# Second-product tiles of the MLPs: from 13 matmuls over 512 tokens to 24 over 256, with their weight blocks 64 bytes higher

## The reference, cut to what matters

```python
def sq_relu_mlp(h, w1, w2):
    a = jax.nn.relu(h @ w1)      # 1024 -> 4096
    return (a * a) @ w2          # 4096 -> 1024, added to x
```

## Time and profile before

| what | value |
|---|---|
| median of 3 runs | 2172.73 us (2171.98 to 2174.36) |
| the profiled execution | 2172.76 us, of which the traced span is 2171.0 us |
| PE | 2157.3 us busy (99%), 12440 matmuls |
| PEld | 1860.9 us (86%), 12440 loads |
| DVE / ACT / POOL | 1494.3 us (69%) / 998.5 us (46%) / 14.5 us (1%) |
| mean granted PE clock | 0.998 |

### The profile page before, as it was taken

The page is one execution under the profiler, slowest core; times in us unless marked ns, Lnnn a source line. Parts: engine busy times, 40 slices in busy tenths (PEclk is TensorE's granted clock), DMA queues, the critical chain, the costliest instruction groups (busy, mean ns, idle before and its releaser), DMA issues.

```text
span 2171.0 us, 32587 instructions
## 1 busy us (share of the span) xinstructions
PE 2157.3 (99%) x12440; PEld 1860.9 (86%) x12440; DVE 1494.3 (69%) x2518; ACT 998.5 (46%) x1724; POOL 14.5 (1%) x14
## 2 busy tenths in 40 slices
PE   9999999999999999999999999999999999999998
PEld 8887888888778888888898899998888888899997
DVE  5866665558666567586666777776887658777775
ACT  5445533434446344375554544444434435444444
POOL 0000000000000000200000000000000000000000
PEclk9999999999999999999999999999999999999999
DMA  5655443335645433464354333333233213333331
GB/s 199 184 176 164 152 128 106 113 122 180 190 138 155 127 103 113 132 181 153 117 155 137 97 98 98 117 98 104 91 92 112 88 49 100 102 100 107 98 114 52
DMA packets 136699, 268.21 MB, mean 124 GB/s; under 512 B 21773, under 2 KB 79931, under 8 KB 136160
## 3 DMA queue, kind: packets, MB, share of 16 engines
q1 hardware_dynamic: 136544, 266.13, 39.7%
HBM read 235.37 MB, written 26.77 MB: 121 GB/s over the span
## 4 chain that ended last, share of the span: by engine, by line
PE 98%; DVE 1%; ACT 0%; issue 0%; DMA 0%; DVEq 0%; SPq 0%; ACTq 0%
PE ps L2348 30%; PE ps L2349 30%; PE ps L2354 29%; PE ps L2369 2%; PE ps L2380 2%; PE ps L2352 1%; PE ps L2351 1%; PE ps L2404 0%; PE ps L2406 0%; PE ps L2394 0%; PE ps L2405 0%; PE ps L2393 0%; PE ps L2392 0%; PE ps L2423 0%; DVE t_X L3066 0%
## 5 line engine op out<-in xcount | busy, mean ns | idle before, releaser
L2348 PE MATMUL ps<-t_P0H,t_whi 128*128 128x512 f32 (+1 forms) x1072 | 419.0, 391 | 1.8 <-DVE t_P0L L2716 1.8
L2349 PE MATMUL ps<-t_P0L,t_whi 128*128 128x512 f32 (+1 forms) x1072 | 413.0, 385 | 0.0
L2354 PE MATMUL ps<-t_P0H,t_wlo 128*128 128x512 f32 (+1 forms) x1044 | 403.2, 386 | 0.0
L2671 DVE TENSOR_TENSOR t_wlo<-t_raw,t_whi 128x1024 fp32r<-128x1024 f32 (+1 forms) x262 | 308.9, 1181 | 40.6 <-PE ps L2354 29.2
L2495 ACT ACTIVATE t_whi<-t_raw 128x1024 fp32r<-128x1024 f32 (+1 forms) x267 | 270.8, 1021 | 83.2 <-PE ps L2354 82.0
L2348 PEld LDWEIGHTS ps<-t_P0H,t_whi 128*128 128x128 f32 x1072 | 201.7, 188 | 54.2 <-issue 14.0
L2349 PEld LDWEIGHTS ps<-t_P0L,t_whi 128*128 128x128 f32 x1072 | 201.9, 188 | 39.2 <-issue 1.0
L2354 PEld LDWEIGHTS ps<-t_P0H,t_wlo 128*128 128x128 f32 x1044 | 196.5, 188 | 40.2
L2348 PE MATMUL ps<-t_P1H,t_whi 128*128 128x512 f32 (+1 forms) x516 | 195.6, 379 | 1.6 <-DVE t_P1L L3054 1.0
L2349 PE MATMUL ps<-t_P1L,t_whi 128*128 128x512 f32 (+1 forms) x516 | 194.1, 376 | 0.0
L2354 PE MATMUL ps<-t_P1H,t_wlo 128*128 128x512 f32 (+1 forms) x500 | 189.5, 379 | 0.0
(11 more groups left out here) (381 smaller groups left out, 4701.7 us busy)
## 6 DMA issues: line engine op xcount, KB each, us to landing
t_raw<-in_wts SPq DMA_DIRECT2D x362, 512.0 KB, 3.6
far<-t_Tb SPq DMA_DIRECT2D x26, 384.0 KB, 3.2
far<-t_Tb SPq DMA_DIRECT2D x16, 512.0 KB, 3.6
t_PTX<-far SPq DMA_DIRECT2D x64, 96.0 KB, 3.5
t_raw<-in_wts SPq DMA_DIRECT2D x16, 384.0 KB, 3.2
t_QKV<-far SPq DMA_DIRECT2D x32, 128.0 KB, 2.7
t_raw<-in_wts SPq DMA_DIRECT2D x13, 256.0 KB, 2.9
t_PTX<-far SPq DMA_DIRECT2D x24, 128.0 KB, 2.8
```

The source lines that it names most:

```text
L2348: e.matmul(s.out, s.sh, s.mh, start=s.first, stop=False, skip_group_check=again)
L2349: e.matmul(s.out, s.sh, s.ml, start=False, stop="halved" in s, skip_group_check=again)
L2354: i = e.matmul(s.out, s.sl, s.mh, start=False, stop=s.end, skip_group_check=again)
L2671: e.tensor_tensor(s.dst, s.raw, s.hi.bitcast(F32), ALU.subtract).then_inc(*mark("lo", s.j))
```

## The change: what it does

A new generator, `gemm_two`, takes the place of `gemm_fm(..., halved=True)` for the 104 tiles. It goes twice over the four steps, first for tokens 0 to 255, then for 256 to 511, both into the same bank, so that a tile is 24 matmuls of 256 columns; the step that marks the tile done hangs on the last of them. The weights of these tiles get tiles of their own, t_WMH and t_WML, which lie over t_MH and t_ML, 64 bytes higher; t_MH and t_ML stay where they were for the other stages that use them. The `halved` path itself stays for the convolution layer.

```diff
+    def gemm_two(src, w, parts, evac, last=True):
+        bank, free = G.take()
+        p = tile()
+        for h in range(2):
+            c = slice(256 * h, 256 * h + 256)
+            for n, (b, t) in enumerate(parts):
+                end = n == len(parts) - 1
+                emit("mm", out=bank[:, c], sh=w.hi(b), sl=w.lo(b), mh=src.hi[:, t, c], ml=src.lo[:, t, c],
+                     first=n == 0, end=end, free=free if h == 0 and n == 0 else [], need=w.ready(n) + src.tok[t],
+                     tile=p if h == 1 and end else None)
+                if h:
+                    tick()
+                yield
+        if last:
+            w.done(p)
+        finish(bank, p, evac)
...
-            return gemm_fm(P1, w, [(4 * d + k, 4 * (c % 2) + k) for k in range(4)], evac, last=d == 1,
-                           halved=halved)
+            return (gemm_two if two else gemm_fm)(P1, w, [(4 * d + k, 4 * (c % 2) + k) for k in range(4)], evac,
+                                                  last=d == 1)
...
-            MHs.give(T["MH"][:, 4 * i:4 * i + 4, :].rearrange("p a b -> p (a b)"), *mfree)
-            MLs.give(T["ML"][:, 4 * i:4 * i + 4, :].rearrange("p a b -> p (a b)"), *mfree)
+            MHs.give(T["WMH"][:, 4 * i:4 * i + 4, :].rearrange("p a b -> p (a b)"), *mfree)
+            MLs.give(T["WML"][:, 4 * i:4 * i + 4, :].rearrange("p a b -> p (a b)"), *mfree)
...
-                run(second_tile(c2, m2 + i, u[f"w{i // 2}"], i % 2, halved=True))
+                run(second_tile(c2, m2 + i, u[f"w{i // 2}"], i % 2, two=True))
...
+    put("WML", [128, 8, 256], F32R, put("WMH", [128, 8, 256], F32R, at[0] - 16384 + SHIFT_M) + 8192)
```

More of the change, by code:

```diff
@@ L25 @@
 WIDE = 1040
-SHIFT_E3, SHIFT_P0, SHIFT_MEM = 64, 64, 192
+SHIFT_E3, SHIFT_P0, SHIFT_MEM, SHIFT_M = 64, 64, 192, 64
 QA, KA, VA, FA, ZA = 0, 256, 512, 768, 772
@@ L1709, in first_tile, with second_tile @@
             return gemm_fm(PS, w, parts8(), evac)
-        def second_tile(c, m, w, d, halved=False):
+        def second_tile(c, m, w, d, two=False):
             def evac(bank, p):
```

## The result

The change makes the kernel slower: 2181.47 us (median of 5 runs, 2180.93 to 2181.88) against 2171.98 us before (median of 5, 2170.67 to 2174.36), a ratio of 1.0043 with a 95% interval of 1.0032 to 1.0055. Forecast were 2170.6 us and a range of 2168.3 to 2174.0. The rival of the wrong pace had named 2182.

What follows compares the result with a forecast made beforehand. PE was taken as the bound, busy 2157.3 of 2171.0 us. Per tile 2.72 + 0.005 + 0.012 = 2.737 against 2.757 gains 0.020, times 104 = 2.1 us: 2172.73 to 2170.6 us, range 2168.3 to 2174.0.

Steps and rivals of the forecast that it cites:

- The rival of the wrong pace: In the 104 tiles: the new pairing misses the 0.1133 pace; 2182 us at 0.118, 2187 at 0.120; chance 0.10.
- What bounds the kernel: In the pairs: PE is busy throughout, so time is the number of matmuls times the distance between their starts.
- The matmuls: Inside each tile: 24 matmuls of 256 columns at the products' 0.1133 us take 2.72 us, replacing 2.74 us.
- Entry: At the tile's start: one block read at offset 128 costs 0.005 us, bounded by nothing and 0.025.
- Exit: Behind the tile: one block read at offset 0 beside the last slice costs 0.012 us, bounded by nothing and 0.023.
- The sum: Per tile 2.737 us instead of 2.757, a gain of 0.020, times 104 = 2.1 us.
- What is late next: Outside PE's matmuls: nothing else pays; DVE, ACT and SP keep rows and order, tightest hand-over has 0.8 us left.
- A price of each half: In the tiles: 11 added fixed prices of 0.014 us, giving 2187 us; counted in the wrong pace's chance of 0.10.
- the 2.9 us estimated from it: For the tiles, by N/2.4 + 2.5 ns: 2.62 us after against 2.59 before, 2.9 us slower in all.
- That the boundaries are free: At tile entry and exit: no cost, so 0.037 us gained per tile, 3.9 us, 2168.8 us; chance 0.17.

Runs made afterwards that it cites:

- the four forms: Changed kernel with a pair's four tiles made different: all halves; first step 512 wide; a later step 512 wide; only the first matmul 512 wide. 2178.76 us.
- the run with one odd block: Low stream kernel plus one extra matmul at each of the 104 tiles' heads, its block 64 bytes above the grid, read once at distance 128; 2180.57 us.
- extra matmul on the grid: Changed kernel plus one 256-column matmul at each of the 104 tiles' heads, past a block at the common tile start, so no distance of 128; 2192.75 us.
- low stream: Changed kernel with weight blocks back on the grid, MLP activations streamed from own tiles 64 bytes lower, all second-product tiles in halves; 2167.65 us.
- first wide: Changed kernel with the first matmul of every one of the pairs' tiles 512 columns wide and the 22 others in halves; 2181.26 us.
- low stream with the tile as before: Low stream kernel with the 104 tiles among the pairs back to 11 matmuls of 512 columns and 2 of 256; 2180.77 us.
- the blocks on the grid: Changed kernel, tiles still in halves, with their weight blocks back at offset 0 instead of 64; 2184.98 us.
- low stream with blocks 64 higher: Low stream kernel with its weight blocks 64 bytes above the grid, so distance 128 throughout the tiles; 2181.89 us.

## Why the prediction was wrong

**What bounds the kernel: right.** PE fills the pairs before and after, and nothing waits.

**The matmuls: the step that failed.** "At the products' pace 24 x 0.1133 = 2.72 us ... I take 0.1133" is the term that was mis-sized: the pace is 0.1177, the tile 2.823 us, 0.103 more than the 2.72 forecast, times 104 = 10.7 us. The reason given, that the distance is that of the products, was half of it: it makes 0.1133 possible, as the four forms show at the very addresses of the change, but 0.1177 is possible at that distance too.

**Entry: the mechanism was missing, not a price.** As a price, 0.005 was right: the step into the tile takes 0.118. But the bounds, nothing to 0.025, took the boundary for a few odd steps behind which the chain returns to its pace. It returned so in the run with one odd block, but not here. What the change does at its boundary is to move both the block and the slice up by 64 bytes. A distance of 128 in between is not needed for it (extra matmul on the grid), and without the move the loss is gone (low stream). The move is not all that counts: behind the same move a first matmul of 512 columns keeps the good pace (first wide), and without any move a tile of 512 columns sends the product behind it to 0.1177 (low stream with the tile as before).

**Exit: too low.** 121 + 122 + 116 + 114 is 0.020 above four steps of 0.1133, as before; 0.012 was taken on the ground that half the cause was gone. With the blocks on the grid, where the whole tile stands at offset 0, the four steps are the same, so their price doesn't hang on how many matmuls stand at that offset. They vanish in the low stream, where neither slices nor blocks move; where only the blocks move, from distance 128 back to 64 (low stream with blocks 64 higher), the four are 117, 123, 118 and 113, again 0.018 too long.

**The sum.** 2.823 + 0.020 = 2.843 instead of 2.737; against 2.757 that is 0.086 per tile, 8.9 us for 104, where the span grew by 8.7 and the medians by 9.5.

**What is late next: right.** Busy times of DVE and ACT are those of before, PE waits for nothing.

**The rivals.** The wrong pace was the right one, at a chance of 0.10. The earlier trace rows had shown two settled paces of one pair of tiles at one distance, 0.118 and 0.1135, and that was the evidence to weigh most. What stood against it, that the products come in from the tiles 104 times and are at 0.1133 four steps later, does not hold in general: behind a fast tile in first wide and in the four forms the same products stay at 0.1177 to their end. A price of each half is refuted by the low stream. The rule of the Trainium skill that was set beside it (page "TensorE: Matmul & The Clock Gate", section "Back-to-back issue gap") is given there for a single isolated matmul, not for a chain with a load to each, so the 2.9 us estimated from it say little here; the rows exceed it by 4% at 256 columns and 5% at 512. That the boundaries are free was true, but of another arrangement: 20.40 us per pair came with it.

**What stays open.** Why distance 64 has two paces, and why the move by 64 bytes turns 0.1133 into 0.1177 at one boundary and back at the next, no run here tells; nor do the loads tell the two apart: in the change, the low stream and first wide they start 2 to 5 ns behind a matmul's start at either pace. The starts only show that a pace, once entered, was held to the next boundary in every tile and product seen.

## What to carry to other kernels

Where PE is the bound, read the distance of its starts in every chain past the first five steps, and compare equal shapes: two settled values for one shape mean a pace to be won, and an address difference that goes with the better one may be necessary without being sufficient. Lay out all tiles that take turns in one chain so that the streamed slices share one place modulo 512 bytes and the loaded blocks another, so that nothing moves where one product follows the other, and keep the matmuls at one width: with 512-column tiles between the products the same layout took 2180.77 us instead of 2167.65. A price bounded by "a few odd steps" is too narrow a bound for a boundary, if the trace shows anywhere that a chain can settle at another pace.

## What the runs showed of the hardware that was not expected

At 2.4 GHz, one load per matmul and no wait, the distance between matmuls of 256 columns depends on the distance of block and slice modulo 512 bytes: 0.120 us at 0, 0.1133 or 0.1177 at 64, 0.1185 in a beat of five at 128 (and the same two as at 64 where t_MEMH streams past t_whi). For 512 columns it is 0.226 at 0 and 0.233 or 0.234 at 64, so that the better distance for the one width is the worse for the other. At 64 both paces of 256 columns keep themselves up over 23 steps, at the same addresses, in one kernel. The Trainium skill, page "TensorE: Matmul & The Clock Gate", section "Step-by-step: what each phase is for", describes the two reads of the array as independent ports, by which a load takes no bandwidth from the running matmul; these runs speak against it: the change and the halves on the grid differ in nothing but where the loaded blocks lie, and a tile takes 2.823 against 2.861 us.
